# One table set for logarithm and exponential on ScalarE, loaded by the kernel itself

## What is computed

```python
u = modulate(rmsnorm(h, norm_mix_g[l]), sh1, sc1)
...
h = h + g1[:, None, :] * mixed
u2 = modulate(rmsnorm(h, norm_ffn_g[l]), sh2, sc2)
h = h + g2[:, None, :] * moe_ffn(u2, ...)
...
return rmsnorm(h, final_norm_g)
```

```python
y = xf * lax.rsqrt(jnp.mean(xf * xf, axis=-1, keepdims=True) + eps)
```

## Time and profile before

| | us |
|---|---|
| median of 3 runs | 2762.91 |
| lowest, highest | 2761.85, 2763.42 |
| the profiled execution's own time | 2763.88 |
| its span, first to last instruction | 2762.3 |
| TensorE busy | 2588.6 (94%) |
| VectorE busy | 1217.0 (44%) |
| ScalarE busy | 721.4 (26%) |

### The profile page before, as it was taken

One profiled execution on the slowest core, in us unless ns is written; L12 is line 12 of the kernel. 1 busy time (PEld: TensorE's weight loads), 2 busy tenths in 40 slices (PEclk: granted clock), 3 DMA queues, 4 the chain that ended last, 5 costly groups with the idle time before them and its releaser, 6 DMA issues. The chain is left out here.

```text
span 2762.3 us, 43676 instructions
## 1 busy us (share of the span) xinstructions
PE 2588.6 (94%) x17760; PEld 1690.1 (61%) x17760; DVE 1217.0 (44%) x2567; ACT 721.4 (26%) x1202; POOL 166.1 (6%) x128
## 2 busy tenths in 40 slices
PE   8999999999999899898999879999999998999997
PEld 3666666588765567566666538747877444555543
DVE  4666565757543222122222157416776224444422
ACT  2333332101113111111111111225554312444421
POOL 0000000000000022222222200000000000000000
PEclk9999999999999999999999989999999999999999
DMA  6222221243322789999998833431111311111110
GB/s 266 107 92 77 77 80 39 111 183 140 135 95 77 301 305 389 383 345 396 329 395 321 292 140 110 149 137 45 49 49 57 114 76 41 61 62 46 46 54 30
DMA packets 81430, 428.24 MB, mean 155 GB/s; under 512 B 16176, under 2 KB 16688, under 8 KB 38096
## 3 DMA queue, kind: packets, MB, share of 16 engines
q1 hardware_dynamic: 53296, 368.47, 34.0%
q0 software_dynamic: 18096, 37.80, 5.3%
q10 hardware_dynamic: 9840, 19.17, 1.9%
HBM read 394.88 MB, written 58.79 MB: 164 GB/s over the span
## 5 line engine op out<-in xcount | busy, mean ns | idle before, releaser
L284 PE MATMUL psum_all<-u,weights 128*128 128x512 f32 x720 | 314.6, 594 | 0.0
L284 PEld LDWEIGHTS psum_all<-u,weights 128*128 128x128 f32 x720 | 135.9, 191 | 162.0 <-issue 161.5
L1811 PE MATMUL psum_all<-weights,big 128*64 128x256 f32 (+2 forms) x1296 | 193.5, 402 | 12.0 <-DMA weights<-t_experts 12.0
L1811 PE MATMUL psum_all<-big 128*32 128x256 f32 (+2 forms) x1648 | 193.9, 382 | 9.5 <-DMA big<-t_experts 7.6
L954 PE MATMUL psum_all<-big,weights 128*128 128x256 f32 x768 | 176.3, 381 | 2.1 <-ACT sq L990 1.3
L1811 PEld LDWEIGHTS psum_all<-weights,big 128*64 128x64 f32 (+2 forms) x1296 | 135.5, 150 | 54.5 <-issue 20.6
L1811 PEld LDWEIGHTS psum_all<-big 128*32 128x32 f32 (+2 forms) x1648 | 136.4, 132 | 42.7 <-issue 11.6
L954 PEld LDWEIGHTS psum_all<-big,weights 128*128 128x128 f32 x768 | 144.7, 190 | 27.4 <-issue 5.1
L1846 DVE COPY big<-psum_all 128x256 f32<-128x256 f32 x46 | 19.5, 425 | 290.0 <-PE psum_all L294 290.0
L954 PE MATMUL psum_all<-big 128*128 128x256 f32 x624 | 141.8, 380 | 0.0
L284 PE MATMUL psum_all<-weights,u 128*128 128x256 f32 x640 | 139.6, 379 | 0.0
(11 more groups left out here) (443 smaller groups left out, 4015.1 us busy)
## 6 DMA issues: line engine op xcount, KB each, us to landing
big<-t_experts SPq DMA_DIRECT2D x96, 1024.0 KB, 28.2
weights<-t_experts SPq DMA_DIRECT2D x96, 1024.0 KB, 23.9
weights<-t_ada SPq DMA_DIRECT2D x24, 1024.0 KB, 7.1
weights<-t_rkvg SPq DMA_DIRECT2D x16, 1024.0 KB, 8.2
rwkv_inputs<-big ACTq DMA_DIRECT2D x48, 256.0 KB, 2.1
big<-rwkv_inputs SPq DMA_DIRECT2D x8, 1280.0 KB, 6.1
weights<-t_x SPq DMA_DIRECT2D x8, 1024.0 KB, 4.8
weights<-t_BC SPq DMA_DIRECT2D x8, 1024.0 KB, 5.1
```

Of the source, the lines that this page charges most:

```text
L284: last = pe.matmul(out, lhsT, rhs, start=n == 0, stop=n == len(terms) - 1)
L1811: ins = pe.matmul(K.psum[rows, bank, n * F_E:(n + 1) * F_E], xT[:, k, rows], X.part(r, n, KD, F_E)[:, k, :], start=k == 0, stop=k == KD - 1)
```

## The change

The spare one-column logarithms and their buffer go.

```diff
-        self.eps, self.logs, self.log_at = self.stat[:, 24:28], self.stat[:, 40:60], 0
+        self.eps = self.stat[:, 24:28]
...
+LN_AND_EXP = 6
+def ln_and_exp(K):
+
+    K.nc.scalar.add_instruction(mybir.InstLoadActFuncSet(act_func_set_id=LN_AND_EXP, name=K.nc.get_next_instruction_name(),
+                                                         engine=mybir.EngineType.Activation))
+
+
+def act_rstd(K, q, name, table=True):
 
 
     act = K.nc.scalar
+    if table:
+        ln_and_exp(K)
     act.wait_ge(*K.eps_here)
-    act.activation(K.logs[:, K.log_at:K.log_at + 1], K.eps[:, 0:1], ACT.Ln, bias=K.eps[:, 0:1]).then_inc(*q.act.tick())
-    K.log_at += 1
     act.wait_ge(*q.pe.at(name, "sum", KD - 1))
...
 def join_root(K, q, name, b, eps):
 
     act = K.nc.scalar
-    act.activation(K.logs[:, K.log_at:K.log_at + 1], K.eps[:, 0:1], ACT.Ln, bias=K.eps[:, 0:1]).then_inc(*q.act.tick())
-    K.log_at += 1
+    if name == "next":
+        ln_and_exp(K)
     act.wait_ge(*q.pe.at(f"{name} mean"))
...
     for j in range(2):
         evict(G_, j, j % 4, ACT.Silu)
+    ln_and_exp(K)
     pair_act(K, XP, qp, 0)
     for j in range(2, 4):
         evict(G_, j, j % 4, ACT.Silu)
+    ln_and_exp(K)
     ln_act(K, XP, qp, 0)
     length_act(K, XP, qp, 0)
     expm_act(K, XP, qp, 0)
     for j in range(4, KD):
         evict(G_, j, j % 4, ACT.Silu)
+    ln_and_exp(K)
...
-        act_rstd(K, q, "pre")
+        act_rstd(K, q, "pre", False)
...
     act.activation(X.gate[0], K.psum[:, 7, :], ACT.Silu).then_inc(*q.act.tick("gate", 0))
+    ln_and_exp(K)
...
         act.activation(X.gate[f % 2], K.psum[:, 7, :], ACT.Silu).then_inc(*q.act.tick("gate", f))
+        ln_and_exp(K)
```

More of the change, by code:

```diff
@@ L351, in act_square @@
     act.activation(K.sq[k % 2][:, :], src, ACT.Square, scale=D ** -0.5).then_inc(*q.act.tick(name, "square", k))
-def act_rstd(K, q, name):
+LN_AND_EXP = 6
[3 more added lines that the diff above has]
+def act_rstd(K, q, name, table=True):
     act = K.nc.scalar
+    if table:
+        ln_and_exp(K)
     act.wait_ge(*K.eps_here)
-    act.activation(K.logs[:, K.log_at:K.log_at + 1], K.eps[:, 0:1], ACT.Ln, bias=K.eps[:, 0:1]).then_inc(*q.act.tick())
-    K.log_at += 1
     act.wait_ge(*q.pe.at(name, "sum", KD - 1))
```

## The result

The changed kernel took 2739.49 us, the median of 3 runs (2735.96 to 2740.72), against 2762.91 before: ratio 0.9905, 95% interval 0.9878 to 0.9932. The forecast was 2745.6, with a range from 2741.0 to 2750.5. The profiled execution took 2735.96 us (span 2734.7); the difference of the two spans is 27.6 us.

What follows compares the result with a forecast made beforehand. TensorE, busy 94% of the span, was taken as the bound, so loads cost only where it or the final chain waits; 9.0 + 1.3 + 3.4 + 2.6 + 1.0 = 17.3 us saved gave 2745.6, range 2741.0 to 2750.5.

Steps and rivals of the forecast that it cites:

- Roots, Exp's load: At seven whole-row roots with somebody waiting behind Exp, the load between Ln and Exp goes, 1.28 us each: 9.0 us.
- Roots, Ln's start: At the roots Ln starts earlier without the small logarithm: 0.2 us at five, 0.3 at "pre", together 1.3 us.
- Pairs: Two loads go per step; first step gains 1.2 us, second 0.8, five others 0.28 each: 3.4, bounds 2.6 and 9.0.
- Attention: Nothing inside the heads; at the end two TensorE idle waits, 1.94 and 1.76 us, get shorter: 2.6 us together.
- Clock: Shorter idle stretches at six places may remove slow products at the lower clock: 1.0 us, bounds -2.4 and +5.
- (a): Rival: the pairs give the whole load, 9.0 us for 3.4, so 2740.0 us; chance 0.08.
- (b): Rival: gains at "ffn" and "next" are lost to transfers, no clock gain, one slow stretch added: 2751.8 us; chance 0.12.
- (c): Rival: a later pass still puts a load ahead of every Ln and Exp, about 2762 us; chance 0.03.
- (d): Rival: each table switch holds a hidden drain, another 1.3 us at nine bare loads, 2734 us; chance 0.01.
- (e): Rival: the new set's load takes longer than 1.28 us at five roots; slower, 2769 us at 6 us more; chance 0.03.

Runs made afterwards that it cites:

- before_again: The kernel before, unchanged, run and traced again: median 2760.0 us over 12 runs, ratio 0.9993.
- fill_idle: The changed kernel with unread products in TensorE's waits behind four roots, six at three of them and four at one: 2742.4 us, ratio 0.9932.
- pairs_var_ahead: The changed kernel with one more load in each of the eight pair steps, ahead of the wait before the variance's Ln: median 2743.92 us.
- after_third: The changed kernel, unchanged, traced a third time; measured once more beside the later runs it had 2743.96 us, ratio 0.9936.

## Why the prediction was wrong, step by step

The mechanism, bare loads between Ln and Exp, was right. What failed were the size of the clock term and a range that had no room for the scatter of executions.

- **Roots, Exp's load, 9.0.** Right. Ln's end to Exp's start went from 1.31 to 0.02, and TensorE's waits behind the roots came back by 1.3 each with the load. The time of that kernel agrees (9.2 by the medians) but is too coarse to show it.
- **Roots, Ln's start, 1.3.** Right in size: the stretches of "ffn", "post" and "ple" fell by 1.46 each, "pre" by 1.5, "next" by 1.28.
- **Pairs, 3.4.** The mechanism was right, the size a little low: the whole stretch fell by 4.2 us (mean of four traces with the old loads in the pairs, 338.8, and of the three of the changed kernel, 334.6). The named waits gave 3.8: L2871 2.6, and L2888 1.2, 5.7 us in eight waits becoming 4.5 in seven. The term read its steps a little wrong, with errors that cancel: VectorE's step from L3526 to L3496 was 1.89 us once and 0.97 six times before and is 0.60 in all seven after, so the first step gave 1.28, each of the others 0.37 (not 0.28, since L3508 starts 0.08 before L3538 ends when nothing holds it) and the second nothing like 0.8. The bounds held the whole.
- **Attention, 2.6.** Right, and so were its two parts. TensorE's waits for the same two products fell from 1.94 to 0.66 and from 1.76 to 0.38, the 0.7 and 0.4 of the forecast. The first of them in the changed kernel, and the wait that follows it:

```profile
2585.68 0.71 PE L284 MATMUL psum_all<-big 128*128 128x128 f32 x4 [0.66 <-ACT big L4080]
2590.68 0.94 PE L284 MATMUL psum_all<-big 128*128 128x128 f32 x6 [1.03 <-ACT big L4080]
```

  The wait of 1.03 is not new. The first trace of before doesn't show it, because there the products ahead of it ran slow and filled it (3.4 us at 0.50 behind the wait of 1.94); before_again, without a slow stretch there, has it:

```profile
2602.24 0.71 PE L284 MATMUL psum_all<-big 128*128 128x128 f32 x4 [1.94 <-ACT big L4067]
2607.24 0.94 PE L284 MATMUL psum_all<-big 128*128 128x128 f32 x6 [1.04 <-ACT big L4067]
```

  So the end of the attention took 37.76 us with the old loads and no slow stretch, and 35.11 with the new: 2.65. With a slow stretch it took 38.05 to 38.82 (three traces), 0.3 to 1.1 more; that is all that the clock adds here.
- **Clock, 1.0.** This is the term of the sum that was mis-sized. I had one such price and took it at two fifths, with six places where idle time shrinks. The traces show "next" 0.7 beyond its wait, the inputs behind it 0.5, "pre" 0.8, the attention's end 0.4: 2.4 us, by the means over all traces in which the stretch is of the one or the other kind. These means are rough, since a slow stretch is there or not: "next" took 22.66 in two traces of the new kind and 24.14 to 24.44 in five, and 25.69 to 26.04 with the old loads; "pre" scatters from 37.2 to 39.9 in the new kind. The term was within its bounds. With the measured sizes the sum is 10.1 for the roots, 4.2, 2.7 and 2.4, together 19.4 for the forecast's 17.3. The other 1.7 to 1.9 us of the 21.1 to 21.3 by the medians are in no stretch that can be named, and lie within the scatter.
- **The range.** This is why the time fell outside it. The forecast with the measured sizes would be some 2743.5, inside the range; the rest of the way to 2739.49 is luck of three executions, for which the range had no room. I took the 1.6 us between the three runs of before as the scatter and left it out, though the prediction itself says that a measurement can tell some 5.5 us. Executions of one and the same kernel differ by 17 us (before: 2756.9 to 2773.9 on one chip), and the median of the first three was 2 to 3 us off. An estimate from that: a range for the median of three runs needed some 3 us on either side besides the bounds. 2741.7, the median of 15, lies inside the range that was given.
- **Rivals.** (a) is out by the traces: the pairs gave 4.2, not 9.0, though the time of the first three runs is just (a)'s 2740.0, which shows how little a time near a rival's says. (b) as it was priced, 2751.8, is out; but its first half, that the experts give back what "ffn" gained, is open: they took 742.2 us on average in the four traces with the old root "ffn" (739.9 to 743.9) and 743.9 in the nine with the new one (741.1 to 745.1). (c), (d) and (e) are out by the rows above; the new set's load takes 1.28.
- The experts and the mixer remain the largest scatter, 2 to 5 us each from trace to trace of one kernel. The first mixer took 848.8 to 851.4 us in the three traces with the old root "mix" and 845.5 to 851.1, on average 848.9, in the eleven with the new one, so a shift of up to 1.5 us by that root is not excluded. What decides where the lower clock falls there was not tried.

## What to carry to other kernels

Look for who starts when the second of two table-bound functions has ended; here a load there cost its full 1.3 us where nothing else was waited for (the roots), 0.37 where VectorE had other work first (the pairs), and nothing where it queued ahead of a wait. Where a wait of TensorE gets shorter, the slow products behind it may go with it, and that gain is the uncertain one. Compare waits by the product that waits, not by the longest in the list, and over more than one trace: a slow stretch can fill a later wait, so that it seems new when the stretch is gone. Before a range is drawn around a forecast of under 1%, find out how far executions of the same kernel differ; three that agree do not show it.

## What was not expected of the chip

Two traces hold one stretch of 27.3 us at the lower clock that does not follow a long wait: fill_idle, and pairs_var_ahead, both at the end of the pairs. Busy time by stretch in pairs_var_ahead, ahead of it and within it (the clock is the number after POOL's):

```profile
2090.00:2116.00 26.00, 24.45 (x695) 21.80 (x691) 14.36 (x37) 11.94 (x19) 0.00 (x0) 1.00 0.35 130
2118.00:2142.00 24.00, 21.19 (x118) 9.43 (x117) 6.84 (x27) 0.00 (x0) 0.00 (x0) 0.54 0.00 1
```

The clock fell at 2119.7. TensorE had been busy 24.45 of the 26 us up to 2116 at full clock, and behind that it had a wait of 0.97 us and one of 0.40, as the changed kernel has them without such a stretch. The pairs' stretch took 298.7 us there for 287. 27.3 us at half the clock cost up to 13.7 us of products and lower the mean clock by 27.3 x 0.5 / 2763 = 0.005. That is just the distance of before's executions at 2769 to 2771 us (mean clock 0.971) from those around 2760 (0.976). So the long stretch would explain them, but none of these was traced: argued, not shown. There is a rival: the time at the lower clock in short stretches differs too, 114.7 us in all in the first trace of after and 143.9 in after_third, which has no long one and took 10.5 us longer. Since it was seen in a kernel without fillers as well, they did not bring it on.
